# Order of the expert block: the first down slice ahead of the second gated half and the next rows

## The chip, the cores and the metric

The kernel runs on one core of a Trainium2 chip. The metric is the device time in microseconds (us), the median of several executions. One more execution was recorded by the hardware profiler; all durations below come from that one.

## The reference, cut to what matters

One layer of a hybrid encoder on a float32 input of 2048 tokens by 1024 channels: two token mixers, their gated merge and output projection, and then a mixture of experts. Only the last part is touched by the change. A router gives each token two of 32 experts; the assignments are sorted by expert and padded to blocks of 128 rows, and each block is computed as

```python
    def expert_block(args):
        xr, e = args
        return (jax.nn.silu(xr @ w1[e]) * (xr @ w3[e])) @ w2[e]
```

`xr` is 128 x 1024, `w1[e]` and `w3[e]` are 1024 x 512, `w2[e]` is 512 x 1024. The results are weighted and added onto the rows of their tokens.

## The kernel before, in words

Each float32 matrix product is made of three TensorE passes (`passes3`, L49): a value is split into a rounded part (`_hi`) and the rest (`_lo`), and hi·hi, hi·lo and lo·hi are added up in PSUM. So every operand needs a cast on ScalarE (`copy`, to `_hi`) and a subtraction on VectorE (to `_lo`) before TensorE may read it.

`routing_and_experts` (L1491) writes out by hand, for each engine, one program that the others meet only through semaphores. `all_experts` (L1559) is the loop over the 32 experts; in it a loop with bounds read at run time goes over the blocks of the expert (one, two or three), and calls `rows` once for each block `b`. In the text a *boundary* is the passage from the last block of one expert to the first block of the next.

TensorE's `rows` (L1900) does for a block:

- `up(h, lo, hi)` (L1901): the gate and up products of half `h` of the 512 hidden channels, in four pieces of six matmuls for each half, 48 matmuls in all. Piece `j` waits until `up_split` has counted the piece of the expert's weights.
- `turn_g(h)` (L1911): two 128 x 128 transposes of gated half `h`. It waits for `g_ready`.
- `turn_x(b + 1)` (L1894): eight transposes of the rows of the next block, which GpSimd gathered (`fetch`, L1609). Their completion, `x_turned`, also lets GpSimd gather the block after.
- `down(k)` (L1917): slice `k` of the down product, six matmuls. Slices 0 and 1 read gated half 0, slices 2 and 3 read half 1, so half 1 must be split (`g_split`) before `down(2)`.

The order before is: `up` of half 0, half of `up` of half 1, `turn_g(0)`, the rest of `up`, `turn_x(b + 1)`, `turn_g(1)`, `down(0)` to `down(3)`.

ScalarE's `rows` (L1687) and VectorE's (L1834) follow in orders of their own, which each keeps strictly: ScalarE has `silu(0)`, `take_y(b)` (the result of the block before), casts of the next expert's down weights in between, `round_g(0)`, `silu(1)`, `round_x(b + 1)`, `round_g(1)` and the last down weight cast. VectorE has `gate(0)`, `down_piece` 0 and 1, `split_g(0)`, `down_piece` 2, `gate(1)`, `split_x(b + 1)`, `split_g(1)`, `down_piece` 3. At a boundary both then do `up_weights(e + 1)` (L1674, L1819): the eight pieces of the next expert's up weights. These can't be done earlier, since `ex_wu_hi` and `ex_wu_lo` have one buffer.

SyncE (L1577) loads the weights of 4 MB + 2 MB of the expert after the next, piece by piece: the down pieces when the last `down_piece` of the expert is done, then each up piece when `up_split` says that its buffer is free. Each piece is 512 KB and has one buffer, `ex_w`.

Of the kernel before, what the change touches and what calls it, by code (L numbers as in the profile page):

```python
# [1490 lines left out]
def routing_and_experts(nc, logits, cst, h2_d, w_pieces, ident_d, out, stage):  # L1491

    with ExitStack() as c:
# [79 lines left out]
        def total(eng):  # L1573
            return eng.value_load(blk_tab[0:1, 2 * NE - 1:2 * NE], min_val=NE, max_val=MAXB)
# [69 lines left out]
        @block.scalar  # L1644
        def _(act):
            nc.scalar.preload_act_table(ACT.Exp)
            nc.scalar.copy(tri[:, :], cst[:, C_TRI:C_TRI + P])
            nc.scalar.copy(ones[:, :], cst[:, C_ONES:C_ONES + P]).then_inc(sums_ready, 1)

            def first_up(j):  # L1650
                act.wait_ge(w_in[j], 16)
                nc.scalar.copy(wu_hi[:, j, :], wr[:, j, :]).then_inc(up_rounded, 1)

            def first_down(k):
                act.wait_ge(w_in[KD + k], 16)
                nc.scalar.copy(wd_hi[:, 0, k, :], wr[:, KD + k, :]).then_inc(down_rounded, 1)

            act.wait_ge(exp_in, 1)
            nc.scalar.activation(gs, gs, ACT.Exp).then_inc(exp_out, 1)
            first_up(0)  # L1660
            first_up(1)
            act.wait_ge(exp_in, 2)
            nc.scalar.activation(ed, ed, ACT.Exp).then_inc(exp_out, 1)
            nc.scalar.preload_act_table(ACT.Silu)
            for j in range(2, KD):
                first_up(j)
            for k in range(KF):
                first_down(k)

            def round_x(b):  # L1670
                act.wait_ge(x_turned, b + 1)
                nc.scalar.copy(x_hi[:, :, :], ps_x[:, :, :]).then_inc(x_rounded, 1)

            def up_weights(e, first):  # L1674
                for j in range(KD):
                    act.wait_ge(w_in[j], e * 16 + 16)
                    act.wait_ge(up_used, first * KD + (j + 1))
                    nc.scalar.copy(wu_hi[:, j, :], wr[:, j, :]).then_inc(up_rounded, 1)  # L1678

            def down_weights(e, u, b=None, lo=0, hi=KF):  # L1680
                for k in range(lo, hi):
                    act.wait_ge(w_in[KD + k], e * 16 + 16)
                    if b is not None:
                        act.wait_ge(down_split, b * KF + (k + 1))
                    nc.scalar.copy(wd_hi[:, u, k, :], wr[:, KD + k, :]).then_inc(down_rounded, 1)  # L1685

            def rows(b, first, e, u, more):  # L1687
                def silu(h):
                    act.wait_ge(up_used, b * KD + (KD + QP * (h + 1)))
                    nc.scalar.activation(s[:, h, :], ps_h[:, h, 0, :], ACT.Silu).then_inc(s_ready, 1)  # L1690

                def round_g(h):
                    act.wait_ge(g_turned, b * 2 + (h + 1))
                    nc.scalar.copy(g_hi[:, h * HK:(h + 1) * HK, :].rearrange("p k r -> p (k r)"),
                                   ps_g[:, h, 0:HF]).then_inc(g_rounded, 1)

                silu(0)
                take_y(b)
                if more:
                    down_weights(e + 1, 1 - u, b, 0, 2)  # L1700
                round_g(0)
                if more:
                    down_weights(e + 1, 1 - u, b, 2, 3)
                silu(1)
                round_x(b + 1)
                round_g(1)
                if more:
                    down_weights(e + 1, 1 - u, b, 3, 4)

            def take_y(b):  # L1710

                act.wait_ge(block_done, b + 1)
                act.wait_ge(ix_y_ready, b * 2 + 2)
                act.wait_ge(y_free, b + 1)
                nc.scalar.activation(y[:, :], ps_y[:, :], ACT.Copy, scale=w_rows[:, :]).then_inc(y_read, 1)  # L1715

            round_x(0)
            act.wait_ge(y_clear, 1)
            act.wait_ge(tab_ready, 1)
            all_experts(act, up_weights, rows)  # L1720
            take_y(total(act))

        @block.vector
        def _(dve):
# [90 lines left out]
            def split_x(b):  # L1815
                dve.wait_ge(x_rounded, b + 1)
                nc.vector.tensor_tensor(x_lo[:, :, :], ps_x[:, :, :], x_hi[:, :, :], ALU.subtract).then_inc(x_split, 1)  # L1817
# [7 lines left out]
            def down_piece(n, u, k):  # L1825
                dve.wait_ge(down_rounded, n * KF + (k + 1))
                nc.vector.tensor_tensor(wd_lo[:, u, k, :], wr[:, KD + k, :], wd_hi[:, u, k, :],  # L1827
                                        ALU.subtract).then_inc(down_split, 1)
# [5 lines left out]
            def rows(b, first, e, u, more):  # L1834
                def gate(h):
                    dve.wait_ge(s_ready, b * 2 + (h + 1))
                    nc.vector.tensor_tensor(g[:, h, :], ps_h[:, h, 1, :], s[:, h, :], ALU.mult).then_inc(g_ready, 1)  # L1837

                def split_g(h):
                    dve.wait_ge(g_rounded, b * 2 + (h + 1))  # L1840
                    part = slice(h * HK, (h + 1) * HK)
                    nc.vector.tensor_tensor(g_lo[:, part, :].rearrange("p k r -> p (k r)"), ps_g[:, h, 0:HF],  # L1842
                                            g_hi[:, part, :].rearrange("p k r -> p (k r)"),
                                            ALU.subtract).then_inc(g_split, 1)

                gate(0)
                if more:
                    down_piece(b + 1, 1 - u, 0)
                    down_piece(b + 1, 1 - u, 1)
                split_g(0)  # L1850
                if more:
                    down_piece(b + 1, 1 - u, 2)
                gate(1)
                split_x(b + 1)
                split_g(1)
                if more:
                    down_piece(b + 1, 1 - u, 3)

# [11 lines left out]
        def _(pe):  # L1870
# [23 lines left out]
            def turn_x(b):  # L1894
                pe.wait_ge(x_in, b * 16 + 16)
                for k in range(KD):
                    last = nc.tensor.transpose(ps_x[:, k, :], xg[:, k * P:(k + 1) * P], ident[:, :])
                last.then_inc(x_turned, 1)

            def rows(b, first, e, u, more):  # L1900
                def up(h, lo, hi):  # L1901
                    for q in range(lo, hi):
                        j = h * QP + q
                        pe.wait_ge(up_split, e * KD + (j + 1))
                        for k in (2 * q, 2 * q + 1):
                            cols = slice((k % 2) * F, (k % 2 + 1) * F)
                            last = passes3(nc, ps_h[:, h, :, :].rearrange("p a c -> p (a c)"), x_hi[:, k, :],
                                           x_lo[:, k, :], wu_hi[:, j, cols], wu_lo[:, j, cols], k == 0, k == KD - 1)
                        last.then_inc(up_used, 1)

                def turn_g(h):  # L1911
                    pe.wait_ge(g_ready, b * 2 + (h + 1))
                    for k in range(HK):
                        last = nc.tensor.transpose(ps_g[:, h, k * P:(k + 1) * P], g[:, h, k * P:(k + 1) * P], ident[:, :])  # L1914
                    last.then_inc(g_turned, 1)

                def down(k):  # L1917
                    pe.wait_ge(down_split, first * KF + (k + 1))
                    for m in range(2):
                        cols = slice(m * TC, (m + 1) * TC)  # L1920
                        last = passes3(nc, ps_y[:, cols], g_hi[:, k, :], g_lo[:, k, :], wd_hi[:, u, k, cols],
                                       wd_lo[:, u, k, cols], k == 0, k == KF - 1)
                    if k == KF - 1:
                        last.then_inc(block_done, 1)

                pe.wait_ge(x_split, b + 1)
                up(0, 0, QP)
                up(1, 0, QP // 2)
                turn_g(0)
                up(1, QP // 2, QP)  # L1930
                turn_x(b + 1)
                turn_g(1)
                pe.wait_ge(g_split, b * 2 + 1)
                pe.wait_ge(y_read, b + 1)
                down(0)
                down(1)
                pe.wait_ge(g_split, b * 2 + 2)
                down(2)
                down(3)
# [119 lines left out]
```

## Time and profile before

| | us |
|---|---|
| median of 3 runs | 2780.48 |
| lowest and highest | 2779.88, 2785.07 |
| the profiled execution | 2781.56 |
| its span, first to last instruction | 2779.7 |
| TensorE busy in the span | 2607.9 (94%) |
| VectorE busy | 1636.7 (59%) |
| ScalarE busy | 1491.0 (54%) |

The expert blocks take the last 950 us of the span. "Busy" for TensorE includes overlap of pipelined matmuls; one 128 x 512 matmul is recorded with 0.39 us though the next starts about 0.23 us after it. PEld is the load of the stationary operand. It is recorded on its own and runs one matmul ahead.

### The profile page before, as it was taken

How to read it: one execution, taken by the hardware profiler on the slowest of the kernel's cores; microseconds unless marked ns; L12 is line 12 of the kernel's file. 1: busy time of each engine (PE TensorE's matmuls, PEld its weight loads, DVE VectorE, ACT ScalarE, POOL GpSimd, SP SyncE). 2: the span in 40 equal slices, each digit the busy share in tenths (PEclk: the TensorE clock that was granted, in tenths of full speed). 3: DMA queues.
4: the chain of work that ended last, by engine and by line, in shares of the span. 5: the costliest groups of instructions: out<-in, count | busy, mean ns of one | idle time of the engine just before them, and what ended most of it. 6: DMA issues, size and time to landing. Idle time of an engine off the chain costs nothing. (4 is left out here: it accounts for less than half of the span.)

```text
span 2779.7 us, 41171 instructions
## 1 busy us (share of the span) xinstructions
PE 2607.9 (94%) x13541; PEld 2158.9 (78%) x13542; DVE 1636.7 (59%) x2207; ACT 1491.0 (54%) x2640; POOL 602.5 (22%) x706
## 2 busy tenths in 40 slices
PE   7899899869999999899799999669999999999997
PEld 6787677658887887788679999558788888888886
DVE  4401455358777776677543333479766667766673
ACT  4312676457766666666422122338666667756563
POOL 0000111035444444344000000012222112212121
PEclk9999999989999999999889999879999999999999
DMA  6454334576456635623554343469977778866783
GB/s 181 119 201 150 111 121 132 159 257 203 179 177 210 203 139 165 206 102 118 178 162 135 120 136 104 154 220 384 363 241 240 227 233 319 319 226 227 226 300 75
DMA packets 196352, 536.66 MB, mean 193 GB/s; under 512 B 19928, under 2 KB 70552, under 8 KB 191744
## 3 DMA queue, kind: packets, MB, share of 16 engines
q1 hardware_dynamic: 169616, 432.80, 45.1%
q0 software_dynamic: 26608, 102.17, 13.3%
q8 instruction: 78, 1.28, 0.2%
q14 instruction: 50, 0.41, 0.0%
HBM read 403.36 MB, written 131.53 MB: 192 GB/s over the span
## 5 line engine op out<-in xcount | busy, mean ns | idle before, releaser
L1064 POOL TENSOR_TENSOR sb_sig<-sb_sig,sb_R 128x512 f32<-128x512 f32 (+1 forms) x320 | 340.7, 1065 | 456.6 <-DVE sb_R L1012 456.5
L51 PE MATMUL ex_ps_h<-ex_wu_hi,ex_x_hi 128*128 128x512 f32 x816 | 323.6, 397 | 2.4 <-DVE ex_x_lo L1817 2.4
L53 PE MATMUL ex_ps_h<-ex_wu_hi,ex_x_lo 128*128 128x512 f32 x816 | 319.3, 391 | 0.0
L52 PE MATMUL ex_ps_h<-ex_wu_lo,ex_x_hi 128*128 128x512 f32 x816 | 318.2, 390 | 0.0
L1822 DVE TENSOR_TENSOR ex_wu_lo<-ex_w,ex_wu_hi 128x1024 fp32r<-128x1024 f32 x248 | 285.3, 1216 | 2.6 <-ACT ex_wu_hi L1678 2.2
L1012 DVE TENSOR_TENSOR_SCAN sb_R<-sb_z,sb_R,sb_zeros 128x512 f32<-128x512 f32 x192 | 245.6, 1279 | 56.4 <-ACT sb_z L936 56.0
L1827 DVE TENSOR_TENSOR ex_wd_lo<-ex_w,ex_wd_hi 128x1024 fp32r<-128x1024 f32 x200 | 239.6, 1219 | 51.1 <-ACT ex_wd_hi L1685 51.0
L945 ACT CAST sb_aT_hi<-sb_pst 128x512 fp32r<-128x512 f32 (+1 forms) x320 | 168.3, 526 | 158.7 <-PE sb_pst L1093 155.6
L1678 ACT CAST ex_wu_hi<-ex_w 128x1024 fp32r<-128x1024 f32 x248 | 241.3, 1055 | 10.9 <-DMA ex_w<-in_w_exp 10.0
L1020 DVE TENSOR_TENSOR sb_aT_lo<-sb_pst,sb_aT_hi 128x512 fp32r<-128x512 f32 (+1 forms) x320 | 192.2, 601 | 76.2 <-ACT sb_aT_hi L945 73.7
L935 ACT ACTIVATE sb_sig<-sb_z 128x512 f32<-128x512 f32 (+1 forms) x320 | 172.4, 539 | 88.0 <-PE sb_z L1086 86.6
L1685 ACT CAST ex_wd_hi<-ex_w 128x1024 fp32r<-128x1024 f32 x196 | 201.9, 1058 | 5.5 <-DMA ex_w<-in_w_exp 5.5
L1690 ACT ACTIVATE ex_s<-ex_ps_h 128x256 f32<-128x256 f32 x102 | 39.2, 384 | 289.4 <-PE ex_ps_h L53 288.7
L51 PE MATMUL ip_ps<-h_hi,ip_w_hi 128*128 128x512 f32 x448 | 182.4, 407 | 8.4 <-DVE ip_w_lo L549 8.4
L1093 PE MATMUL sb_pst<-sb_ident,sb_sig 128*128 128x128 f32 x1088 | 171.5, 273 | 16.8 <-DVE sb_aT_lo L1020 16.7
L1093 PEld LDWEIGHTS sb_pst<-sb_ident,sb_sig 128*128 128x128 f32 x1088 | 137.7, 141 | 56.4 <-issue 17.3
L1625 POOL DMA_INDIRECT out_x<-w_stage,ex_ix_y x52 | 85.3, 1640 | 440.0 <-ACT w_stage L1715 440.0
L51 PEld LDWEIGHTS ex_ps_h<-ex_wu_hi,ex_x_hi 128*128 128x128 f32 x816 | 153.6, 188 | 33.1 <-issue 2.8
L53 PEld LDWEIGHTS ex_ps_h<-ex_wu_hi,ex_x_lo 128*128 128x128 f32 x816 | 153.6, 188 | 33.0
L51 PE MATMUL sb_psg<-h_hi,sb_w_hi 128*128 128x512 f32 x384 | 156.3, 407 | 24.3 <-DMA sb_w_lo<-wg_d 12.4
L52 PEld LDWEIGHTS ex_ps_h<-ex_wu_lo,ex_x_hi 128*128 128x128 f32 x816 | 153.9, 189 | 30.7
L53 PE MATMUL ip_ps<-h_hi,ip_w_lo 128*128 128x512 f32 x448 | 175.8, 393 | 0.0
(270 smaller groups left out, 6318.1 us busy)
## 6 DMA issues: line engine op xcount, KB each, us to landing
ex_w<-in_w_exp SPq DMA_DIRECT2D x384, 512.0 KB, 9.1
sb_w_hi<-wg_d SPq DMA_DIRECT2D x48, 512.0 KB, 3.6
sb_w_lo<-wg_d SPq DMA_DIRECT2D x48, 512.0 KB, 4.6
gates<-sb_go SPq DMA_DIRECT2D x64, 256.0 KB, 3.0
mo_gates<-gates SPq DMA_DIRECT2D x64, 256.0 KB, 3.6
h<-mo_rows POOLq DMA_DIRECT2D x17, 512.0 KB, 3.0
nt_x<-in_x SPq DMA_DIRECT2D x16, 512.0 KB, 4.5
vhl<-nt_vo SPq DMA_DIRECT2D x16, 512.0 KB, 5.5
```

Of the source, the lines that this page charges most:

```text
L51: nc.tensor.matmul(out, w_hi, x_hi, start=first, stop=False)
L52: nc.tensor.matmul(out, w_hi, x_lo, start=False, stop=False)
L53: return nc.tensor.matmul(out, w_lo, x_hi, start=False, stop=last)
L935: nc.scalar.activation(sig[:, j % 5, 0:width], z[:, j % 3, 0:width], ACT.Sigmoid, scale=HD ** -0.5)
L1012: nc.vector.tensor_tensor_scan(R[:, r, first + 1:first + width + 1], z[:, j % 3, 0:width], zeros[:, 0:width], start, ALU.mult, ALU.max).th ...
L1020: nc.vector.tensor_tensor(aT_lo[part], ps_t[:, j % 2, b0 * P:TC].rearrange("p (b s) -> p b s", s=P), aT_hi[part], ALU.subtract).then_inc(l ...
L1064: nc.gpsimd.tensor_tensor(sig[:, j % 5, 0:width], sig[:, j % 5, 0:width], R[:, r, first:first + width], ALU.mult).then_inc(a_done, 1)
L1093: last = nc.tensor.transpose(ps_t[:, j % 2, b * P:(b + 1) * P], sig[:, j % 5, b * P - OFF[j]:(b + 1) * P - OFF[j]], ident[:, :])
L1678: nc.scalar.copy(wu_hi[:, j, :], wr[:, j, :]).then_inc(up_rounded, 1)
L1685: nc.scalar.copy(wd_hi[:, u, k, :], wr[:, KD + k, :]).then_inc(down_rounded, 1)
L1822: nc.vector.tensor_tensor(wu_lo[:, j, :], wr[:, j, :], wu_hi[:, j, :], ALU.subtract).then_inc(up_split, 1)
L1827: nc.vector.tensor_tensor(wd_lo[:, u, k, :], wr[:, KD + k, :], wd_hi[:, u, k, :], ALU.subtract).then_inc(down_split, 1)
```

## The change

Three orders are rewritten; no instruction is added or dropped. On TensorE `turn_x(b + 1)` and `turn_g(1)` trade places and `down(0)` goes ahead of both. On ScalarE and VectorE the work on gated half 1 goes ahead of the work on the next rows.

```diff
@@ ScalarE, rows
                 silu(1)
+                round_g(1)
                 round_x(b + 1)
-                round_g(1)
                 if more:
                     down_weights(e + 1, 1 - u, b, 3, 4)
@@ VectorE, rows
                 gate(1)
+                split_g(1)
                 split_x(b + 1)
-                split_g(1)
                 if more:
                     down_piece(b + 1, 1 - u, 3)
@@ TensorE, rows
                 up(1, QP // 2, QP)
-                turn_x(b + 1)
-                turn_g(1)
                 pe.wait_ge(g_split, b * 2 + 1)
                 pe.wait_ge(y_read, b + 1)
                 down(0)
+                turn_g(1)
+                turn_x(b + 1)
                 down(1)
                 pe.wait_ge(g_split, b * 2 + 2)
                 down(2)
```

## Rows read from the trace of the kernel before

**Rows 1.** Busy time by stage: us, engines' busy (instructions), granted clock, DMA share, GB/s

```profile
1854.00:1858.00 4.00, 4.00 (x12) 3.11 (x12) 3.73 (x4) 4.00 (x6) 0.14 (x2) 0.63 0.39 130
1858.00:1990.00 132.00, 128.88 (x602) 105.37 (x601) 116.63 (x121) 105.01 (x127) 32.77 (x35) 1.00 1.03 378
2005.00:2779.00 774.00, 757.78 (x3544) 621.60 (x3542) 505.62 (x555) 467.62 (x597) 149.18 (x213) 0.99 0.72 240
```

**Rows 2.** The waits from 2005 us on: us in total, times, longest

```profile
PEld ex_ps_g L1914 <- DVE ex_g L1837: 12.4, 42, 0.3
```

**Rows 3.** Groups by line, VectorE from 2005 us on

```profile
L1822 DVE TENSOR_TENSOR ex_wu_lo<-ex_w,ex_wu_hi 128x1024 fp32r<-128x1024 f32 x184 | 210.7, 1215 | 0.0
```

**Rows 4.** Timeline, TensorE's matmuls, a block that ends an expert: start, us, what

```profile
2091.23 0.39 PE L53 MATMUL ex_ps_h<-ex_wu_hi,ex_x_lo 128*128 128x512 f32 x1
2091.46 1.03 PE L1897 MATMUL ex_ps_x<-ex_ident,w_stage 128*128 128x128 f32 x8
2092.56 0.44 PE L1914 MATMUL ex_ps_g<-ex_ident,ex_g 128*128 128x128 f32 x2
2098.32 0.39 PE L51 MATMUL ex_ps_h<-ex_wu_hi,ex_x_hi 128*128 128x512 f32 x1
...
2106.48 0.38 PE L1914 MATMUL ex_ps_g<-ex_ident,ex_g 128*128 128x128 f32 x2
2106.93 0.39 PE L52 MATMUL ex_ps_h<-ex_wu_lo,ex_x_hi 128*128 128x512 f32 x1
```

**Rows 5.** The same stretch, TensorE's weight loads

```profile
2092.55 0.20 PEld L1914 LDWEIGHTS ex_ps_g<-ex_ident,ex_g 128*128 128x128 f32 x2 [0.29 <-DVE ex_g L1837]
2098.09 0.19 PEld L51 LDWEIGHTS ex_ps_h<-ex_wu_hi,ex_x_hi 128*128 128x128 f32 x1
2106.25 0.37 PEld L1914 LDWEIGHTS ex_ps_g<-ex_ident,ex_g 128*128 128x128 f32 x2
```

**Rows 6.** The same stretch, ScalarE

```profile
2091.66 0.38 ACT L1690 ACTIVATE ex_s<-ex_ps_h 128x256 f32<-128x256 f32 x1 [1.22 <-PE ex_ps_h L53]
2092.53 1.02 ACT L1672 CAST ex_x_hi<-ex_ps_x 128x1024 fp32r<-128x1024 f32 x1 [0.49 <-PE ex_ps_x L1897]
2093.44 0.38 ACT L1694 CAST ex_g_hi<-ex_ps_g 128x256 fp32r<-128x256 f32 x1
2093.71 1.06 ACT L1685 CAST ex_wd_hi<-ex_w 128x1024 fp32r<-128x1024 f32 x1
```

**Rows 7.** The same stretch, VectorE

```profile
2092.08 0.42 DVE L1837 TENSOR_TENSOR ex_g<-ex_ps_h,ex_s 128x256 f32<-128x256 f32 x1
2093.58 1.22 DVE L1817 TENSOR_TENSOR ex_x_lo<-ex_ps_x,ex_x_hi 128x1024 fp32r<-128x1024 f32 x1 [1.08 <-ACT ex_x_hi L1672]
2094.72 0.41 DVE L1842 TENSOR_TENSOR ex_g_lo<-ex_ps_g,ex_g_hi 128x256 fp32r<-128x256 f32 x1
2095.05 1.22 DVE L1827 TENSOR_TENSOR ex_wd_lo<-ex_w,ex_wd_hi 128x1024 fp32r<-128x1024 f32 x1
2096.19 9.16 DVE L1822 TENSOR_TENSOR ex_wu_lo<-ex_w,ex_wu_hi 128x1024 fp32r<-128x1024 f32 x8
2105.27 0.41 DVE L1837 TENSOR_TENSOR ex_g<-ex_ps_h,ex_s 128x256 f32<-128x256 f32 x1
```

**Rows 8.** Timeline, a load and matmuls after a wait, at the lower clock

```profile
1832.95 0.29 PEld L51 LDWEIGHTS ex_ps_h<-ex_wu_hi,ex_x_hi 128*128 128x128 f32 x1 [2.84 <-issue]
1833.55 0.63 PE L52 MATMUL ex_ps_h<-ex_wu_lo,ex_x_hi 128*128 128x512 f32 x1
1833.97 0.63 PE L53 MATMUL ex_ps_h<-ex_wu_hi,ex_x_lo 128*128 128x512 f32 x1
```

**Rows 9.** Timeline, end of the first block; the block that ends at 2007 us

```profile
1852.44 0.20 PEld L1914 LDWEIGHTS ex_ps_g<-ex_ident,ex_g 128*128 128x128 f32 x2 [4.05 <-DVE ex_g L1837]
1855.41 2.35 DVE L1822 TENSOR_TENSOR ex_wu_lo<-ex_w,ex_wu_hi 128x1024 fp32r<-128x1024 f32 x2
...
2002.52 0.20 PEld L1914 LDWEIGHTS ex_ps_g<-ex_ident,ex_g 128*128 128x128 f32 x2 [0.96 <-DVE ex_g L1837]
```

## The prediction, made before the changed kernel was run

> **What bounds the kernel now.** I read the busy time by stage first, then the waits, then the timeline of one block on each engine, since an order within a block can only be judged there. The expert phase has three parts [rows 1]. From 2005 us to the end TensorE is busy 757.8 of 774 us at a granted clock of 0.99 (the 2.4 GHz level), with DMA at 0.72: TensorE's stream of matmuls sets the end. From 1858 to 1990 us DMA is at 1.03 with 378 GB/s: the experts have one block each there and the weight transfers set the pace. From 1854 to 1858 us DMA is at 0.39 and the clock at 0.63: the transfers run dry after the first block, because the buffers of the next weights are not yet free.
>
> In the last part the only thing that TensorE waits for is `turn_g(1)`: 42 times, 12.4 us, 0.3 us at most [rows 2]. The weight load of that transpose sits idle for 0.29 us before 2092.55, until `gate(1)` on VectorE, which runs from 2092.08 to 2092.50, is done [rows 5, 7]. So `turn_x` hides `silu(1)` and `gate(1)` except for 0.29 us. VectorE splits 184 pieces of up weights after 2005 us, eight to a boundary, so there are 23 boundaries among the 42 blocks [rows 3].
>
> **What the change takes away.** I count from 2091.46, where the matmul that follows `up` begins [rows 4]. Matmuls follow each other at 0.227 us (2091.23 to 2091.46 with its rounding). `down(0)` is six, 1.36 us. It needs only half 0, long split. `gate(1)` is ready at +1.04 and a load sees it about 0.06 us later, at +1.10; TensorE now wants the load of `turn_g(1)` at 1.36 - 0.23 = +1.13. The 0.29 us are covered, with almost nothing to spare for the load but 0.26 us for the matmul. The number of switches between transposes and matmuls is the same. Gain 42 x 0.29 = 12.2 us; ends 0.25 and 0.33 us for each, 10.5 to 13.9. The wait for `g_split` before `down(2)` has slack: `turn_g(1)` ends near +1.8, cast and subtraction take 0.4 us each, so half 1 is split at about +2.7, and `down(2)` comes at +4.0.
>
> **What it moves.** `turn_x` begins later by `down(0)`, 1.36 us, and `turn_g(1)`, 0.22 us (2106.48 to 2106.93, less one step) [rows 4]: at +1.58 = 2093.04. Behind it hangs a chain that goes on to the next expert's weights:
>
> - `round_x`, 1.07 us after `turn_x` begins (2091.46 to 2092.53) [rows 4, 6]: 2094.11.
> - `split_x`, 1.05 us after `round_x` begins (2092.53 to 2093.58) [rows 6, 7]: 2095.16.
> - `down_piece` 3, next on VectorE, 1.14 us on (2093.58 to 2094.72): 2096.30. Its cast on ScalarE follows `round_x` by 0.91 us and takes 1.06: done at 2096.08, in time.
> - `up_weights`, 1.14 us on (2095.05 to 2096.19): 2097.44. Before it was 2096.19 [rows 7]. It is 1.25 us late, not 1.58, as `split_g(1)` with its 0.33 us has gone ahead into idle time.
>
> Both queues are in order, so nothing gets round this: what stands behind the later `round_x` and `split_x` is the last down piece and all eight up pieces.
>
> **Within an expert** that costs nothing: `split_x` is done at +4.92 and the next block starts at +6.57. **At a boundary** TensorE waits for the first up piece. Before, it was ready at 2096.19 + 1.22 = 2097.41 and its load was issued at 2098.09 [rows 5, 7]: 0.62 us of slack after 0.06 us of latency. Now the piece is ready at 2098.66, the load can go at 2098.72, and TensorE, 0.29 us ahead, wants it at 2097.80: late by 0.92 us. A matmul stream that waited catches up a little. At the 1.2 GHz level, load to second matmul is 0.60 us after a wait instead of two steps of 0.42 [rows 8]; I take half of these 0.25 us for the full clock, 0.12. So the stall is 0.80 us. Bounds 0.65 (the transposes start 0.1 us sooner, more is caught up) and 0.92. The later pieces don't stall: VectorE makes one in 1.14 us (9.16 us for eight), TensorE uses one in 1.36.
>
> The delay shows once more. `gate(0)` of the next block begins behind the eight pieces, at 2105.27 before, hence at 2106.52, and is done at 2106.93; the load of `turn_g(0)` could go at 2106.99. TensorE wants it at 2106.25 - 0.29 + 0.80 = 2106.76 [rows 5, 7]. 0.23 us late, about 0.10 us of stall; bounds 0 and 0.2. From there ScalarE, which follows TensorE, leads again.
>
> For a boundary 0.90 us, 23 of them 20.7 us. Against 12.2 us of gain: **+8.5 us** after 2005 us. Said for a pair of blocks of one expert: 0.58 us gained, 0.90 lost.
>
> **Before 2005 us.** In the first block TensorE is idle for 4.05 us before `turn_g(1)` [rows 9], of which `down(0)` would fill 1.36. But the end of this block also frees the buffers for the weights that run dry. `turn_g(1)` goes at 1852.45 as before, `turn_x` at 1852.67, and by the chain (1.07, 1.05, 1.14, 1.14) the up pieces start at 1857.07 instead of 1855.41: 1.7 us later. The transfer-bound stretch starts that much later and moves the same bytes at the same rate, so it ends up to 1.7 us later, less what small gaps give back. In its last block the load of `turn_g(1)` waits 0.96 us [rows 9], so `gate(1)` is there about 1.8 us after `up`; with `down(0)` done meanwhile some 0.5 us of the block is saved. The later requests in between find the queues full (1.03), 1.25 us of 18 should not drain them. I take +0.8 us; bounds -1 and +3.
>
> **Sum.** 8.5 + 0.8 = +9.3 us on the profiled execution, 2781.56 to 2790.9 us; its span would be about 2789. That execution was 1.1 us above the median of 2780.48, so I forecast **2789.8 us**. The bounds together give 23 x 0.65 - 13.9 - 1 = 0 and 23 x 1.12 - 10.5 + 3 = +18.3. For this kernel 0.2%, or 5.6 us, is about the least change that a measurement tells from none.
>
> **The rivals.**
>
> *The cover holds at the boundary too (faster).* If the first up piece were still in time, only the gain is left: 2780.5 - 12.2 + 0.8 = 2769.1 us. It decides at a delay of `up_weights` below 0.33 us (slack 0.62 less 0.29). For it: no wait of TensorE for up pieces appears in [rows 2], so the slack is real, and blocks inside experts do gain. Against it: each link is a dependence with a measured length, and they add up to 1.25. Chance 0.10.
>
> *The two cancel.* A stall near 0.55 us for a boundary, a little below my bound, with no stall at `gate(0)`: 2780.5 + 12.7 - 12.2 + 0.8 = 2781.8 us. It decides if the transposes start earlier than their order says, or a waiting stream catches up by more than at the lower clock. Chance 0.15.
>
> *The transfers lose too (slower still).* If the later `down_piece` 3 lets the queues run dry at the eight boundaries before 2005 us, each adds up to 1.25 us: 2789.8 + 10 = 2799.8 us. Against it is the full share of DMA; for it, that SyncE asks for no up piece before the last down piece is split. Chance 0.06.
>
> *It does not do what it says.* If `gate(1)` is later than +1.4 in every block, because `silu(1)` or the down pieces are late, `down(0)` covers no more than `turn_x` did: 2780.5 + 20.7 + 0.8 = 2802.0 us. VectorE's times in [rows 7] give 0.26 us of room. Chance 0.03.
>
> *The transposes hold TensorE for their whole duration (slower by far).* Two are recorded with 0.38 us and eight with 1.03 [rows 4], which makes steps of 0.11 and 0.27 for one. If those behind `down(0)` could not overlap, `turn_x` would take 8 x 0.27 = 2.16 us instead of 0.88 and the chain to the next weights would be 1.28 us later: 23 x 1.28 = 29 us more, 2819 us. Against it stands the overlap in the same row. Chance 0.02.
> The Trainium skill, TensorE: Matmul & The Clock Gate, Part 4: PE-mode transpose, gives about 275 ns for a transpose in a kernel's context; spent one after another this is that rival, and the trace disagrees, with eight in 1.03 us.
>
> **How the numbers follow.** The forecast has 0.64, its own range 2786 to 2797 us. The range for 8 in 10 adds the cancelling case and part of the next two: 2777 to 2798 us. Slower by more than 0.2%: 0.64 + 0.06 + 0.03 + 0.02, less 0.03 of the forecast's own lower edge, 0.72. Within 0.2%: 0.15 + 0.03 = 0.18. Faster: 0.10.
>
> **What would show each step.** The wait of the load of `turn_g(1)` for `gate(1)` goes from 42 x 0.29 us to about none after 2005 us. The step from block to block, now 18.0 us (72 matmuls at 0.227, `turn_x` with its wait 1.1, twice `turn_g` 0.22, and some 0.1 for the restart), becomes 17.7 us inside an expert and 18.6 us across a boundary. `up_weights` starts 5.4 us after `gate(1)` instead of 4.11. A new wait of about 0.8 to 0.9 us stands in front of the first load of `ex_ps_h` at 23 boundaries, released by the first `ex_wu_lo`, and DVE's gate releases `turn_g(0)` there. If `up_weights` starts less than 4.5 us after `gate(1)`, or the first load does not wait, the forecast is wrong; if the end of the transfer-bound stretch moves by more than 3 us, the early part is.

## The result, and the profile after

| | us |
|---|---|
| median of 6 runs, changed kernel | 2793.81 (2791.72 to 2795.16) |
| median of 6 runs, kernel before | 2781.51 |
| ratio, 95% interval | 1.0039 (1.0028 to 1.0050) |
| forecast | 2789.8, range 2777 to 2798 |

The change makes the kernel slower by 0.39%, 10.8 us (7.8 to 13.9). The ratio is not the quotient of the two medians, which lie 12.3 us apart. The forecast was 9.3 us over the profiled execution before; the median came 4.0 us above the forecast, inside its range. The profiled execution took 2793.72 us with a span of 2791.9. I take its trace in the order in which the prediction named its steps.

First the waits of TensorE from 2005 us on, as in [rows 2] (us in total, times, longest):

```profile
PEld ex_ps_h L51 <- DVE ex_wu_lo L1822: 19.8, 21, 1.0
PE ex_ps_h L51 <- DVE ex_wu_lo L1822: 12.2, 23, 0.6
PEld ex_ps_g L1914 <- DVE ex_g L1837: 6.1, 28, 0.3
```

The one old wait was for `gate` 42 times. Now the larger wait is of a new kind: the first matmul of `up` waits for the first piece of the next expert's weights, 23 times, once for each boundary (two of the 23 idle loads, 1.0 us each, stand in the list as "issue"). What is left for `gate` is `turn_g(0)` behind each of the 23 boundaries, as the next view shows, and five times `turn_g(1)`, below 0.2 us each.

The same block as in [rows 4 to 7], the fourteenth, with the `gate(1)` of the blocks on either side of it. VectorE:

```profile
2079.11 0.42 DVE L1837 TENSOR_TENSOR ex_g<-ex_ps_h,ex_s 128x256 f32<-128x256 f32 x1
...
2096.81 0.42 DVE L1837 TENSOR_TENSOR ex_g<-ex_ps_h,ex_s 128x256 f32<-128x256 f32 x1
2098.38 0.42 DVE L1842 TENSOR_TENSOR ex_g_lo<-ex_ps_g,ex_g_hi 128x256 fp32r<-128x256 f32 x1 [1.15 <-ACT ex_g_hi L1694]
2099.90 1.22 DVE L1817 TENSOR_TENSOR ex_x_lo<-ex_ps_x,ex_x_hi 128x1024 fp32r<-128x1024 f32 x1 [1.09 <-ACT ex_x_hi L1672]
2101.04 1.22 DVE L1827 TENSOR_TENSOR ex_wd_lo<-ex_w,ex_wd_hi 128x1024 fp32r<-128x1024 f32 x1
2102.18 9.16 DVE L1822 TENSOR_TENSOR ex_wu_lo<-ex_w,ex_wu_hi 128x1024 fp32r<-128x1024 f32 x8
2111.27 0.41 DVE L1837 TENSOR_TENSOR ex_g<-ex_ps_h,ex_s 128x256 f32<-128x256 f32 x1
...
2115.39 0.42 DVE L1837 TENSOR_TENSOR ex_g<-ex_ps_h,ex_s 128x256 f32<-128x256 f32 x1
```

TensorE's loads and matmuls:

```profile
2103.45 0.19 PEld L51 LDWEIGHTS ex_ps_h<-ex_wu_hi,ex_x_hi 128*128 128x128 f32 x1 [0.95 <-DVE ex_wu_lo L1822]
2111.73 0.20 PEld L1914 LDWEIGHTS ex_ps_g<-ex_ident,ex_g 128*128 128x128 f32 x2 [0.22 <-DVE ex_g L1837]
```
```profile
2097.56 0.38 PE L1914 MATMUL ex_ps_g<-ex_ident,ex_g 128*128 128x128 f32 x2
2097.78 1.03 PE L1897 MATMUL ex_ps_x<-ex_ident,w_stage 128*128 128x128 f32 x8
2103.45 0.50 PE L51 MATMUL ex_ps_h<-ex_wu_hi,ex_x_hi 128*128 128x512 f32 x1 [0.53 <-DVE ex_wu_lo L1822]
2103.79 0.40 PE L52 MATMUL ex_ps_h<-ex_wu_lo,ex_x_hi 128*128 128x512 f32 x1
```

`turn_g(1)` no longer waits here. `up_weights` starts 2102.18 - 2096.81 = 5.37 us after `gate(1)`; it was 4.11 [rows 7]. The first load of `up` waits 0.95 us, and it goes 0.05 us after the first piece (1.22 of the 9.16 us) is split. From `gate(1)` to `gate(1)` it is 17.70 us inside the expert (2079.11 to 2096.81) and 18.58 us across the boundary (2096.81 to 2115.39).

Over all blocks the two numbers hardly move: the median of 18 steps inside an expert is 17.70 us, of 23 steps across a boundary 18.58; before, both were 18.02. Four of the 23 are longer, 18.70, 18.82, 18.83 and 19.30 us. In the block at their end `down(0)` itself starts late: its load is idle for 0.16 to 0.63 us. It needs half 0, and in the longest one VectorE reaches `split_g(0)` late, behind two down pieces that it takes late; the cast of an up piece had waited 0.54 us for its transfer just before. From `gate(1)` of block 9 to that of block 50 (blocks counted from 0), 41 steps, the kernel before took 738.78 us (2020.06 to 2758.84), the changed one 746.86 (2024.24 to 2771.10): +8.08 us.

The rest of the 12.2 us between the two spans lies ahead of block 9. 1.69 us of it are there before the first expert block starts (the first `turn_x` is at 1830.26 instead of 1828.57). That is not the change: in the ten traces of this study that moment falls anywhere from 1826.95 to 1832.78 us. The other 2.49 us come between the first `turn_x` and block 9. 0.49 us of these lie ahead of `gate(1)` of block 0, where the two kernels still do the same (23.40 us before, 23.89 after; 23.40 to 24.39 in the ten traces). From there to block 9 it is 168.09 us before and 170.09 after: the change's own part is 2.00 us.

### The profile page after: what moved, and what is told of

It reads as the page before. It is cut to its first block and busy times, and to the rows that moved or that the text cites. A ratio compares the mean times of both kernels' runs of the same rounds, so it can differ in the third digit from the quotient of the medians.

```text
span 2791.9 us, 41171 instructions
## 1 busy us (share of the span) xinstructions
PE 2612.6 (94%) x13541; PEld 2156.6 (77%) x13542; DVE 1637.9 (59%) x2207; ACT 1495.3 (54%) x2640; POOL 611.6 (22%) x706
## 5 line engine op out<-in xcount | busy, mean ns | idle before, releaser
L1827 DVE TENSOR_TENSOR ex_wd_lo<-ex_w,ex_wd_hi 128x1024 fp32r<-128x1024 f32 x200 | 239.5, 1218 | 35.3 <-ACT ex_wd_hi L1685 35.1
L52 PE MATMUL ip_ps<-h_lo,ip_w_hi 128*128 128x512 f32 x448 | 175.7, 392 | 0.0
```

Source lines behind the costliest of these rows:

```text
L52: nc.tensor.matmul(out, w_hi, x_lo, start=False, stop=False)
```

## The experiments

Each ran beside the kernel before on the same chip; the ratios are to it. The time of the kernel before was 2783.37 us in the first four and 2784.62 us in the last four. "Early" below is the time from the first `turn_x` to `gate(1)` of block 9: 191.49 us before, 193.98 after. "Late" is from there to block 50: 738.78 and 746.86. A difference in "early" below 1 us says nothing, by the spread just named. The expectations start from 2781.5 us for the kernel before, or from 2793.8 and 2767.7 us for the two kernels that were varied, while the kernel before took 2 to 3 us more than 2781.5 beside these runs. So a time 1 to 3 us outside an expected range means little by itself.

### The last down piece goes first

The `if more:` around each of the moved lines is left out here.

```diff
 ScalarE            silu(1)
+                   down_weights(e + 1, 1 - u, b, 3, 4)
                    round_g(1)
                    round_x(b + 1)
-                   down_weights(e + 1, 1 - u, b, 3, 4)
 VectorE            gate(1)
+                   down_piece(b + 1, 1 - u, 3)
                    split_g(1)
                    split_x(b + 1)
-                   down_piece(b + 1, 1 - u, 3)
```

> The changed kernel, with the last down piece (its cast on ScalarE, its subtraction on VectorE) put ahead of the work on gated half 1, so that it leaves the chain to the next expert's weights and fills the idle time after gate(1). TensorE's order is that of the changed kernel. Theory (the loss is the late first up piece): up_weights starts 4.2 us after gate(1) instead of 5.37, its first piece is ready 0.2 us before TensorE wants it, the wait at the 23 boundaries goes and only the gain of 0.29 us for each block is left: 2781.5 - 12.2 = 2769 us, 2768 to 2772. Rival (TensorE's new order itself, or the transfers, cost the time): no better than the changed kernel, about 2793 us.

Measured: 2767.71 us, ratio 0.9944 (0.9931 to 0.9958), 15.6 us faster than before and 0.3 us below the expected range. VectorE at a boundary:

```profile
2094.21 0.42 DVE L1837 TENSOR_TENSOR ex_g<-ex_ps_h,ex_s 128x256 f32<-128x256 f32 x1
2095.15 1.23 DVE L1827 TENSOR_TENSOR ex_wd_lo<-ex_w,ex_wd_hi 128x1024 fp32r<-128x1024 f32 x1 [0.51 <-ACT ex_wd_hi L1685]
2096.29 0.42 DVE L1842 TENSOR_TENSOR ex_g_lo<-ex_ps_g,ex_g_hi 128x256 fp32r<-128x256 f32 x1
2097.30 1.23 DVE L1817 TENSOR_TENSOR ex_x_lo<-ex_ps_x,ex_x_hi 128x1024 fp32r<-128x1024 f32 x1 [0.59 <-ACT ex_x_hi L1672]
2098.44 9.17 DVE L1822 TENSOR_TENSOR ex_wu_lo<-ex_w,ex_wu_hi 128x1024 fp32r<-128x1024 f32 x8
```

The down piece sits where VectorE was idle, `up_weights` starts 4.23 us after `gate(1)`. The wait for `ex_wu_lo` is gone from the list of waits, and all 41 late steps are 17.70 us: late 725.70, 13.1 us less than before. TensorE's order is exactly the changed kernel's. So that order gains, and what lost the time is the lateness of one chain on the other engines.

### One move alone: `turn_x` stays first

```diff
 TensorE, kernel before
                    turn_x(b + 1)
-                   turn_g(1)
                    pe.wait_ge(g_split, b * 2 + 1)
                    pe.wait_ge(y_read, b + 1)
                    down(0)
+                   turn_g(1)
                    down(1)
```

> The kernel before, with one move only: down(0) goes between turn_x(b+1) and turn_g(1). ScalarE and VectorE keep their old orders. Theory: down(0) covers gate(1) as in the change, turn_x and the chain behind it stay where they were, up_weights starts some 4.55 us after gate(1) (its last down cast waits for round_g(1), 0.4 us) and the first up piece is at most 0.1 us late: 2781.5 - 12.2 + 0 to 2 = 2769 to 2771.5 us. Rival (transposes in the middle of the down product cost TensorE time, or the later half 1 stalls down(2)): above 2781 us. By the theory half 1 is split at 3.7 us after up and down(2) wants it at 3.7 us, so up to 0.1 us a block could be lost there, 4 us in all.

Measured: 2773.57 us, ratio 0.9961 (0.9948 to 0.9975), 10.9 us faster. The time lies 2 us above the expected 2769 to 2771.5, the gain inside the 10 to 12.5 us that this meant. `up_weights` starts 4.56 us after `gate(1)`; no boundary stall. The steps are 17.81 us, both kinds, but for two of 18.45 and 18.87; late 730.77. The 0.11 us more than above is the price that the expectation had named, of half 1 for `down(2)`:

```profile
PEld ex_ps_y L51 <- issue: 8.7, 43, 0.2
```

The cause is given as "issue", yet the place (`ex_ps_y`) and the count (43) fit the wait in front of `down(2)`, which comes once in a block. In one block read through, VectorE has split half 1 at 2113.18 us and the load goes at 2113.31, after 0.20 us idle.

### The kernel before, made late at the boundary

```diff
 VectorE, up_weights
                     dve.wait_ge(up_rounded, e * KD + (j + 1))
+                    if j == 0:
+                        nc.vector.tensor_tensor(wu_lo[:, j, :], wr[:, j, :], wu_hi[:, j, :],
+                                                ALU.subtract).then_inc(twice, 1)
+                        dve.wait_ge(twice, e * 1)
```

> The kernel before, all orders old, but VectorE does the subtraction of the first up piece twice at each boundary, the first time to no use: up_weights is late by 1.28 us as it is in the changed kernel (1.25), and nothing else is touched. Theory: the slack of 0.62 us is used up, a stall of 0.54 us at the first load and 0.1 us at turn_g(0), 23 times: +14.7 us after 2005 us and +1 to 2 us before: 2797 us, 2792 to 2800. Rival (the late piece is harmless, the loss of the changed kernel is elsewhere): 2781 to 2784 us.

Measured: 2796.42 us, ratio 1.0047 (1.0031 to 1.0062), 13 us slower. The subtraction that counts, the second, is L1827 in this kernel. With all orders old, the changed kernel's new wait appears:

```profile
PEld ex_ps_h L51 <- DVE ex_wu_lo L1827: 13.7, 21, 0.7
PE ex_ps_h L51 <- DVE ex_wu_lo L1827: 5.5, 23, 0.3
```

Boundary steps 18.58 us, others 18.01: 1.25 us of lateness (2098.56 instead of 2097.31 for the piece that counts) cost 0.57 us, since 0.6 us of slack came first. Here the loss of the changed kernel is made without the change.

### The changed kernel, made late by the same

The same edit in the changed kernel.

> The changed kernel, and VectorE does the subtraction of the first up piece twice at each boundary (1.28 us later, as in the same edit of the kernel before). Theory: the changed kernel has no slack left there, so the whole 1.28 us are paid at each boundary (in the kernel before the same edit cost 0.56): the step across a boundary goes from 18.58 to 19.86 us, 23 x 1.28 = +29.4 us after 2005 us, and some +6 us before, where the step passes the 19.0 us of the transfers: 2829 us, 2820 to 2833. Rival (some slack is left, the stall that is seen is only a follower of something else): +13 us as in the kernel before, 2807 us.

Measured: 2835.85 us, ratio 1.0171 (1.0153 to 1.0189). Against the changed kernel (1.0039) that is 1.3%, 37 us. Boundary steps are 19.83 us, others 17.72: the 1.25 us are paid in full. The time is 3 us above the expected range. Late takes 32.9 us more than in the changed kernel (779.77 against 746.86) where 23 x 1.25 us would be 28.8: three of the boundary steps take 21.4 us, 4.7 us too much together. Early takes 9.0 us more where some 6 had been expected. What makes the three steps long was not looked into.

```profile
PEld ex_ps_h L51 <- DVE ex_wu_lo L1827: 46.3, 21, 2.2
PE ex_ps_h L51 <- DVE ex_wu_lo L1827: 41.2, 23, 1.9
```

The two experiments together measure the slack: the same delay costs 0.57 us before and 1.25 us after. What has gone from one kernel to the other, 0.68 us, is all the slack there was (0.62 by the prediction's reading).

### The helpers' orders undone

The changed kernel with the old orders on ScalarE and VectorE (`round_x` before `round_g(1)`, `split_x` before `split_g(1)`).

> The changed kernel's order on TensorE, the old orders on ScalarE and VectorE. Theory: half 1 waits behind round_x and split_x and is split only 5.3 us after up, down(2) wants it at 3.7: a stall of 1.5 us in every block, less the gain of 0.29; up_weights is then in time for the delayed TensorE and the stall at the boundary is gone: 42 x 1.2 = +51 us, and up to 4 us early: 2836 us, 2825 to 2845. Rival (it is the new order of ScalarE and VectorE that costs time): faster than the changed kernel, below 2790 us.

Measured: 2846.77 us, ratio 1.0228 (1.0213 to 1.0244), 63 us slower. Every late step is 19.36 to 19.39 us, with no difference at a boundary. The wait is in front of `down(2)`:

```profile
PEld ex_ps_y L51 <- issue: 77.8, 43, 1.8
PE ex_ps_y L51 <- DVE ex_g_lo L1842: 59.2, 43, 1.4
```

The stall is 1.67 us a block (19.37 - 17.70), where I had said 1.5; early takes 7.9 us more, where I had said up to 4. So the time came 2 us above the expected range. The swap on the two helpers is thus needed by TensorE's new order; it is not what costs.

### The cover taken away

The kernel with the last down piece first, and `down(0)` put back behind `turn_g(1)` and `turn_x(b + 1)`.

> The kernel with the last down piece first, and down(0) put back behind turn_g(1) and turn_x(b+1), so that TensorE has nothing to do between up and turn_g(1). Theory: the load of turn_g(1) is wanted 0.23 us before the end of up and gate(1) is visible 1.10 us after it: late by 1.33 us, less 0.15 caught up, 1.18 us in every block: steps of 18.88 us, 2767.7 + 42 x 1.18 + 1 = 2818 us, 2810 to 2825. This is what any cover is worth; turn_x (0.88 us) left 0.29 to 0.32 of it open. Rival (the gain of the change is not the cover, but the new neighbours of the transposes): near 2768 us.

Measured: 2822.22 us, ratio 1.0124 (1.0107 to 1.0142). All steps are 18.87 us, 1.17 more than with the cover.

```profile
PEld ex_ps_g L1914 <- DVE ex_g L1837: 58.2, 43, 1.4
```

That, 1.35 us for one, is how long the load of `turn_g(1)` waits for `gate(1)` when nothing stands between it and `up`. Eight transposes covered all but 0.32 us of it, six large matmuls cover all.

### The down pieces asked for one by one

```diff
 SyncE
-                sp.wait_ge(down_split, end * KF + KF)
                 for k in range(KF):
+                    sp.wait_ge(down_split, end * KF + (k + 1))
                     load(e + 2, KD + k)
```

In the kernel with the last down piece first:

> The kernel with the last down piece first, and SyncE asks for each down piece when that piece is split, not for all four after the last. Theory (the part before 2005 us is set by how long the transfers run dry after the first block): the pieces asked for earlier fill most of the 4 to 5 us in which nothing is transferred, and the end of the transfer-bound stretch comes that much sooner: 2767.7 - 3.5 = 2764 us, 2762 to 2767. After 2005 us no change. Rival (that stretch is set by the bytes and by TensorE, the dry time does not matter): 2767 to 2769 us.

In the changed kernel:

> The changed kernel with the same edit on SyncE. Theory: the changed kernel lost 2.5 us before 2005 us beside the 8.1 us after it, because its transfers run dry longer (0 GB/s from 1856 to 1860 us). With each down piece asked for by itself this goes and some more: 2793.8 - 4 = 2790 us, 2787 to 2792, and steps after 2005 us stay 17.70 and 18.58. Rival (the 2.5 us is not from the transfers): unchanged, 2793 to 2795 us.

Measured: 2766.02 us, ratio 0.9925 (0.9911 to 0.9939), and 2788.92 us, ratio 1.0017 (1.0007 to 1.0027). The stretch behind the first block, in the changed kernel and in this variant of it (engines, granted clock, DMA share, GB/s):

```profile
1854.00:1858.00 4.00, 4.00 (x17) 3.48 (x17) 1.00 (x3) 1.04 (x2) 0.18 (x1) 0.62 0.10 23
1858.00:1862.00 4.00, 3.49 (x16) 2.53 (x15) 3.62 (x4) 4.00 (x5) 3.43 (x3) 1.00 0.42 118
```
```profile
1854.00:1858.00 4.00, 4.00 (x23) 3.55 (x22) 1.81 (x3) 2.81 (x4) 1.48 (x4) 0.91 0.59 232
1858.00:1862.00 4.00, 3.47 (x16) 2.56 (x15) 4.00 (x4) 4.00 (x5) 2.13 (x2) 1.00 0.73 197
```

The execution of the variant reached these blocks some 1.7 us sooner, so the same clock times are not the same moments. Counted from `gate(1)` of block 0, the transfers moved 15, 125 and 277 GB/s in the first three stretches of 4 us in the changed kernel, and 386, 135 and 283 in the variant: the gap is gone from the first stretch.

Early goes from 193.98 to 191.31 us, and late from 746.86 to 746.02, as the four longer steps are gone (23 boundary steps of 18.54 to 18.61). In the other kernel early goes from 190.63 to 188.51, late stays at 725.70. Counted from `gate(1)` of block 0 to block 9 the edit saves 2.8 us in the changed kernel and 2.0 in the other. That is what the earlier requests are worth there. They are earlier at every boundary; that the gap after the first block is the place is read from the trace, in which the transfers of the changed kernel are full from 1866 us on (1.03, 385 GB/s). The ratios say 5 to 6 us, but each ratio has an interval of 3 to 4 us to both sides. With 2766.02 us the kernel with both edits has the lowest time of the study, 0.75% ahead of the kernel before; its interval still meets that of the kernel with the last down piece first alone (0.9911 to 0.9939, 0.9931 to 0.9958).

## Why the prediction was right, step by step

**The gain of the cover.** Said: 0.29 us a block. Measured: 18.02 to 17.70, 0.32 us. Here the idle time of the load understates what the wait costs, by a tenth; where nothing covers, it overstates it (1.35 us idle, 1.17 of step).

**The chain of the moved `turn_x`.** Said: `turn_x` 1.36 + 0.22 us later, `up_weights` 1.25 us later. Measured: 5.37 - 4.11 = 1.26. `turn_g(1)` to `turn_x` is 0.22 us, and the transposes overlap as before (eight in 1.03 us), so the rival in which they don't has fallen.

**The stall at the boundary.** Said: the load late by 0.92 us, 0.80 of stall, 0.10 more at `turn_g(0)`: 0.90. Measured: idle load 0.95 and 0.22 us, step 18.58 - 17.70 = 0.88 us. Both twice-split kernels confirm that it is this piece, and the slack of 0.6 us.

**The sum after 2005 us.** Said +8.5, measured +8.08. It is a small difference of two larger ones, 23 x 0.88 = 20.2 lost and 41 x 0.32 = 13.1 gained; this makes 7.1. Nearly all of the remaining 1.0 us comes from the four longer steps (19.30 us at most, and three of them followed by one that is 0.15 us shorter or more), which the prediction did not have. The gain was said too low by 0.03 us a block and the loss too high by 0.02 a boundary. So the two terms were right, and that their sum came within 0.4 us of the measured one is luck in part: without the longer steps it would have been 1.4.

**Before 2005 us.** Said +0.8 (-1 to +3), measured +2.49, of which 2.00 us behind `gate(1)` of block 0. This is the term that was mis-sized. I had said that `turn_g(1)` of block 0 goes as before, with `turn_x` right behind it, and the up pieces 1.7 us later. I had also said that `down(0)` needs only half 0, "long split". In block 0 it was not: `down(0)` could begin only when `split_g(0)` was done, at 1852.81, and by then TensorE had been idle for 3.48 us. From 1853.79 on its matmuls come every 0.43 us, at the 1.2 GHz level (granted clock 0.50 from 1854 to 1856), so `down(0)` took until 1855.07 and ended after `gate(1)`:

```profile
1852.94 0.49 PE L51 MATMUL ex_ps_y<-ex_wd_hi,ex_g_hi 128*128 128x512 f32 x1 [3.48 <-DVE ex_g_lo L1842]
1854.64 0.63 PE L53 MATMUL ex_ps_y<-ex_wd_hi,ex_g_lo 128*128 128x512 f32 x1
1855.07 0.63 PE L1914 MATMUL ex_ps_g<-ex_ident,ex_g 128*128 128x128 f32 x2
1855.49 1.81 PE L1897 MATMUL ex_ps_x<-ex_ident,w_stage 128*128 128x128 f32 x8
```
```profile
1852.39 0.42 DVE L1842 TENSOR_TENSOR ex_g_lo<-ex_ps_g,ex_g_hi 128x256 fp32r<-128x256 f32 x1
1854.15 0.42 DVE L1837 TENSOR_TENSOR ex_g<-ex_ps_h,ex_s 128x256 f32<-128x256 f32 x1
1860.67 4.62 DVE L1822 TENSOR_TENSOR ex_wu_lo<-ex_w,ex_wu_hi 128x1024 fp32r<-128x1024 f32 x4
```

Now the chain to the weights runs through these matmuls, where before `turn_x` had been done early. The up pieces start 6.52 us after `gate(1)` of that block; before it was 3.44 (1851.97 to 1855.41). That is 3.1 us later, not 1.7. The 1.4 us beyond the prediction can be read from the rows: `turn_x` starts 1.34 us after `gate(1)` instead of the 0.70 said, and `round_x` begins 1.85 us behind it (1857.34) instead of 1.07.

The transfers stand still meanwhile (0 GB/s from 1856 to 1860 us), and 2.0 us of the delay reach block 9. The loss shows in the first four steps from block to block: 19.63, 18.03, 18.03 and 18.33 us before, 19.73, 18.63, 18.66 and 19.38 after. It is shown that earlier requests give 2.8 us back here; that the lower clock is what made the gap longer than I had said is read from this trace and was not tested by itself.

**The rivals.** "The cover holds at the boundary" did not happen, but the first experiment made it happen, with 2767.7 us for the 2769.1 that I had given it. "The two cancel" is ruled out by the interval, and by 0.88 us at a boundary for the 0.55 that it needed. "The transfers lose too" would have needed a further loss at each of the eight boundaries. The transfers run full from 1864 us on (1.03), there is one gap, and the fifth to eighth steps differ from the old ones by less than 0.1 us. In a small way it did come true behind 2005 us: the longest of the four longer steps follows a late transfer, and with the down pieces asked for earlier all four are gone.

## What to carry to other kernels

When work is moved later on the busiest engine, follow what hangs behind it through the in-order queues of the others to its last user: here the user was the next expert's first weight piece, three instructions and two engines away, and its slack was 0.6 us. A cover is worth only what it covers, 0.3 us a block, while the thing moved to make room costs what exceeds its slack. And when the theory says which instruction is in the way, try taking that one out of the chain: it turned a loss of 0.4% into a gain of 0.6%.

## What the runs showed of the hardware

The start of the expert blocks wanders by up to 6 us between executions of kernels that are the same up to there (1826.95 to 1832.78 us). A comparison of two single spans is blind below that; the steps between blocks, nearly all of which repeat to 0.02 us, are not.

The idle time of a weight load is near what the stall costs, but not equal to it. One load late by 0.95 us and another by 0.22 cost 0.88 us of step together, one late by 1.35 us cost 1.17, and one idle for 0.29 us cost 0.32.
